# Block pair kernel: the second half of the middle norm one unit later and cut in three, its spreads after it, and five weight tiles bounded by a one-column sum on TensorE

## What is computed

```python
    x = x + jnp.einsum('bsf,fd->bsd', f, w_ff2[l])      # end of block 1
    x = rms_norm(x, final_g)                            # middle norm
    # block 2, first layer
    h = _rms(x, norm_g)                                 # a_norm_2
    proj = h @ w_in                                     # 1024 x 4096
    q, k, v, g = jnp.split(proj, [DA_QK, 2 * DA_QK, 2 * DA_QK + DA_V], axis=-1)
    qs = [_rope_partial(_rms(q[:, :, :, c], q_norm), pos) for c in range(2)]
    ks = [_rope_partial(_rms(k[:, :, :, c], k_norm), pos) for c in range(2)]
```

## Time and profile before

| | us |
|---|---|
| time, median of 3 runs | 2532.23 (2521.53 to 2538.52) |
| time of the profiled execution | 2530.41 |
| its span | 2528.6 |
| TensorE busy | 2363.5 |
| VectorE busy | 1519.4 |
| ScalarE busy | 968.2 |
| GpSimd busy | 216.0 |

### The profile page before, as it was taken

One profiled execution on the slowest core, in us unless ns is written; L12 is line 12 of the kernel. 1 busy time (PEld: TensorE's weight loads), 2 busy tenths in 40 slices (PEclk: granted clock), 3 DMA queues, 4 the chain that ended last, 5 costly groups with the idle time before them and its releaser, 6 DMA issues.

```text
span 2528.6 us, 30214 instructions
## 1 busy us (share of the span) xinstructions
PE 2363.5 (93%) x12840; PEld 1252.4 (50%) x12840; DVE 1519.4 (60%) x1962; ACT 968.2 (38%) x1383; POOL 216.0 (9%) x263
## 2 busy tenths in 40 slices
PE   6999999999999999898999777899999998888899
PEld 4445444444444444344444455654444445666764
DVE  6898755644454455777631488965534307888862
ACT  5245334212121212323321466732323116777741
POOL 0001030000000002324201101022000000000000
PEclk9999999999999999898999899999999998999999
DMA  4010011110101010121011000021130100000021
GB/s 177 34 67 34 1 34 63 70 67 34 67 34 67 34 67 34 36 101 67 34 67 34 1 1 1 8 93 34 67 133 34 68 1 34 1 1 1 1 84 50
DMA packets 50326, 116.00 MB, mean 46 GB/s; under 512 B 2386, under 2 KB 7819, under 8 KB 49808
## 3 DMA queue, kind: packets, MB, share of 16 engines
q1 hardware_dynamic: 48456, 105.40, 11.8%
q10 hardware_dynamic: 1736, 8.68, 0.8%
HBM read 101.49 MB, written 12.58 MB: 45 GB/s over the span
## 4 chain that ended last, share of the span: by engine, by line
PE 76%; DVE 13%; ACT 6%; issue 3%; DMA 1%; POOL 1%; ACTq 0%; DVEq 0%; POOLq 0%
PE PS L72 72%; ACT RG L81 4%; PE PS L75 3%; DVE R L93 2%; DVE R L101 2%; DVE RG L107 2%; DVE mx L110 2%; DVE RG L101 2%; ACT OV L84 1%; DVE scl L110 1%; DMA RG<-in_a_w_in 1%; DVE RG L93 1%; DVE oss L110 1%; ACT R L81 1%; ACT OV L81 0%
## 5 line engine op out<-in xcount | busy, mean ns | idle before, releaser
L72 PE MATMUL PS<-R,RG 128*128 128x512 f16 (+1 forms) x5472 | 1167.6, 375 | 10.2 <-DVE RG L101 4.7
L72 PEld LDWEIGHTS PS<-R,RG 128*128 128x128 f16 (+1 forms) x5472 | 543.4, 103 | 631.8 <-issue 14.5
L72 PE MATMUL PS<-RG,R 128*128 128x512 f16 x2880 | 634.6, 381 | 4.5 <-DVE R L101 4.0
L72 PEld LDWEIGHTS PS<-RG,R 128*128 128x128 f16 x2880 | 282.7, 98 | 337.8 <-issue 7.5
L81 ACT ACTIVATE R<-PS,scl 128x512 f32<-128x512 f32 (+1 forms) x192 | 126.8, 687 | 716.1 <-PE PS L72 616.3
L101 DVE SCALAR_TENSOR_TENSOR R<-PS,scl,R 128x512 f32<-128x512 f32 (+1 forms) x208 | 148.7, 746 | 149.2 <-PE PS L72 124.1
L107 DVE TENSOR_TENSOR_SCAN RG<-RG 128x127 f32<-128x127 f32 (+7 forms) x128 | 168.6, 1345 | 110.4 <-ACT RG L81 110.1
L72 PE MATMUL PS<-R,OV 128*128 128x64 f32 (+2 forms) x1456 | 194.5, 286 | 34.9 <-DVE R L93 32.8
L101 DVE SCALAR_TENSOR_TENSOR RG<-RG,scl 128x4096 f16<-128x4096 f32 (+1 forms) x43 | 188.7, 4389 | 52.2 <-ACT RG L81 52.2
L72 PEld LDWEIGHTS PS<-R,OV 128*128 128x128 f32 x1456 | 180.6, 199 | 45.1 <-DVE R L93 39.3
L75 PE MATMUL PS<-ident,RG 128*128 128x128 f32 x864 | 148.5, 289 | 47.1 <-ACT OV L84 23.9
(11 more groups left out here) (120 smaller groups left out, 1546.7 us busy)
## 6 DMA issues: line engine op xcount, KB each, us to landing
RG<-in_w_ff SPq DMA_DIRECT2D x16, 2048.0 KB, 8.1
RG<-in_a_w_in SPq DMA_DIRECT2D x8, 2048.0 KB, 8.5
RG<-in_w_in SPq DMA_DIRECT2D x4, 2048.0 KB, 9.6
xspill<-R ACTq DMA_DIRECT2D x2, 4096.0 KB, 15.3
RG<-in_w_kv SPq DMA_DIRECT2D x4, 2048.0 KB, 8.0
RG<-in_b_w_in SPq DMA_DIRECT2D x4, 2048.0 KB, 7.9
R<-in_x SPq DMA_DIRECT2D x8, 512.0 KB, 9.1
RG<-in_w_out SPq DMA_DIRECT2D x2, 2048.0 KB, 7.7
```

Source lines behind the costliest of these rows:

```text
L72: return self.engine.matmul(*a, **k) if self.engine else Nothing()
```

## The change

1. Spread `final_g` of half 0 leaves the end of block 1 (j = 12) for unit 7; its diagonal goes from j = 11 to unit 5, its eight `final_x` from j = 12, 13 to units 7 and 8.
2. Half 1: sums from unit 1 to 3, spread `a_norm_2` from unit 2 to 4, `final_h` from units 2, 3 (four and four) to units 3, 4, 5 (four, two, two), spread `final_g` from unit 6 to 10, `final_x` from units 6, 7 to 10, 11, the spill from unit 9 to 12.
3. Tile 23 is converted four products later (j = 12 instead of 8).
4. Tiles 24, 25, 26 and 27 are measured and converted at other places. Measurements, before: units 5, 10, 16, 24; after: units 6, 14, 22, 30. Conversions, before: after units 6, 12, 17, 25; after: units 9, 17, 25 and the second vv unit. Tiles 28 and 29 move from the first and second unit of their vv half to the sixth and seventh of the first, and the fourth and fifth of the second.
5. For tiles 24 to 27 and 30 (`BOUNDED`) GpSimd's reduction over the partitions is gone. TensorE multiplies the 128 peaks by `ones` (one column) into a PSUM bank of the ring, which gives their sum in each partition, an upper bound of the largest; VectorE's `power` reads it from there. The factor can be smaller by up to seven bits than before. TensorE does this at the start of the unit at whose end the tile is converted, and waits there for the measurement.

```diff
@@ -174,12 +174,13 @@
 for _i in range(7, 38):
     if _i not in (28, 29):
         MEASURE[_i, 1], CONVERT[_i, 2] = _i + 2, _i + 2
-for _i in (7, 8, 19, 20, 21, 22, 23, 30, 31, 32, 33, 35):
+for _i in (7, 8, 19, 20, 21, 22, 23, 24, 25, 26, 27, 30, 31, 32, 33, 35):
     del MEASURE[_i, 1], CONVERT[_i, 2]
 for _j, _m, _c in ((7, None, (6, 7)), (8, (7, 2), (7, 3)), (9, (7, 6), (7, 7)), (10, (8, 6), (8, 8)),
-                   (21, (19, 1), (19, 2)), (22, (19, 6), (20, 1)), (23, (20, 7), (21, 9)),
-                   (24, (23, 2), (23, 3)), (25, (22, 7), (23, 5)), (32, (30, 7), (30, 8)),
+                   (21, (19, 1), (19, 2)), (22, (19, 6), (20, 1)), (23, (20, 7), (21, 13)),
+                   (24, (23, 3), (22, 6)), (25, (23, 7), (24, 2)), (26, (24, 7), (25, 2)),
+                   (27, (25, 7), (26, 2)), (28, (26, 6), (26, 7)), (29, (27, 4), (27, 5)), (32, (30, 7), (30, 8)),
                    (33, (31, 4), (32, 4)), (34, (32, 8), (33, 1)), (35, (33, 5), (33, 6)),
                    (37, (35, 3), (35, 8))):
     CONVERT[_c] = _j
@@ -187,6 +188,8 @@
         MEASURE[_m] = _j
 LOW = {(_i, _at + 1): _j for (_i, _at), _j in CONVERT.items() if (_i, _at) != (35, 8) and (_i, _at) != (30, 8)}
 LOW[36, 1], LOW[31, 1] = 37, 32
+
+BOUNDED = (24, 25, 26, 27, 30)
 def block_kernel(nc, A):
@@ -492,6 +495,17 @@
                                       start=(k == 0 and ws + hs == 0), stop=(k == 7 and hs == 1))
                 mm.then_inc(*full.up(*key))
                 last_product[i] = key
+
+            def bound(i):
+
+                b = banks.take(("bound", i))
+                e.wait_ge(*sig("w_peak").at(i))
+                e.wait_ge(*banks.free(("bound", i)))
+                e.matmul(b[:, 0:1], ones[:, :], w_col(i, 0), start=True, stop=True).then_inc(*full.up("bound", i))
+
+            def feed(i, use):
+                if CONVERT.get((i, use)) in BOUNDED:
+                    bound(CONVERT[i, use])
             def h_ready(name, n):
@@ -717,8 +731,6 @@
                     sums("final", 0)
                 if j == 8:
                     spread("a_norm_2", 0)
-                if j == 12:
-                    spread("final_g", 0)
                 down(key)
@@ -731,21 +743,25 @@
                 mm.then_inc(*full.up("qt", u))
             for u, (which, c, t) in enumerate(qk_units):
-                if u == 1:
+                if u == 3:
                     sums("final", 1)
-                if u == 2:
+                if u == 4:
                     spread("a_norm_2", 1)
-                if u == 6:
-                    spread("final_g", 1)
+                if u in (7, 10):
+                    spread("final_g", u // 10)
+                feed(22 + 2 * which + c, t + 1)
                 product_n(22 + 2 * which + c, t, ("qk", u), ready=h_ready("a_norm_2", t // 4))
                 if u > 2:
                     qk_turn(u - 3)
             for c in range(2):
                 for t in range(NT):
+                    feed(26 + c, t + 1)
                     product_n(26 + c, t, ("vv", c, t))
                     if c == 0 and t < 3:
                         qk_turn(29 + t)
             for t in range(NT):
+                if t == 2:
+                    bound(30)
                 for c in range(2):
                     product_n(28 + c, t, ("gg", t, c))
@@ -960,10 +976,13 @@
                 e.tensor_reduce(w_col(i, 0), w_raw(i), AX.X, ALU.max,
                                 apply_absolute_value=True).then_inc(*sig("w_peak").up(i))
-            def power(inv, f, top, bits=14):
-
-                e.tensor_scalar(inv, top, TINY, 2.0 ** -bits, ALU.max, ALU.mult).then_inc(*step.up())
-                e.wait_ge(*step.last())
+            def power(inv, f, top, bits=14, key=None):
+
+
+                done = sig("bank_dve") if key else step
+                up = banks.empty([key], done, *key) if key else step.up()
+                e.tensor_scalar(inv, top, TINY, 2.0 ** -bits, ALU.max, ALU.mult).then_inc(*up)
+                e.wait_ge(*done.last())
                 e.tensor_scalar(inv.bitcast(I32), inv.bitcast(I32), EXPONENT, None,
                                 ALU.bitwise_and).then_inc(*step.up())
                 e.wait_ge(*step.last())
@@ -973,6 +992,11 @@
                 return e.scalar_tensor_tensor(low, src, f, high, ALU.mult, ALU.subtract)
             def factor(i):
+                if i in BOUNDED:
+                    key = ("bound", i)
+                    e.wait_ge(*full.at(*key))
+                    power(w_inv(i), w_col(i, 2), banks.ap(key)[:, 0:1], key=key).then_inc(*sig("w_factor").up(i))
+                    return
                 e.wait_ge(*sig("w_top").at(i))
                 power(w_inv(i), w_col(i, 2), w_col(i, 1)).then_inc(*sig("w_factor").up(i))
@@ -1453,10 +1477,6 @@
                     diagonal(("norm2", 1), ("a_norm_2", 0), 8)
                 if 8 <= j < 12:
                     final_h(0, range(2 * j - 16, 2 * j - 14))
-                if j == 11:
-                    diagonal(("a_norm_2", 0), ("final_g", 0), 0)
-                if j in (12, 13):
-                    final_x(0, range(4 * j - 48, 4 * j - 44))
                 down(key, j % 8 + 9)
@@ -1492,15 +1512,20 @@
                                 ALU.subtract).then_inc(*banks.empty([key], sig("bank_dve"), *key))
             for u in range(32):
-                if u == 1:
+                if u == 3:
                     final_factors(1)
-                    diagonal(("final_g", 0), ("a_norm_2", 1), 12)
-                if u in (2, 3):
-                    final_h(1, range(4 * u - 8, 4 * u - 4))
-                if u == 4:
-                    diagonal(("a_norm_2", 1), ("final_g", 1), 4)
-                if u in (6, 7):
-                    final_x(1, range(4 * u - 24, 4 * u - 20))
+                    diagonal(("a_norm_2", 0), ("a_norm_2", 1), 12)
+                    final_h(1, range(4))
+                if u in (4, 5):
+                    final_h(1, range(2 * u - 4, 2 * u - 2))
+                if u == 5:
+                    diagonal(("a_norm_2", 1), ("final_g", 0), 0)
+                if u in (7, 8):
+                    final_x(0, range(4 * u - 28, 4 * u - 24))
+                if u == 8:
+                    diagonal(("final_g", 0), ("final_g", 1), 4)
+                if u in (10, 11):
+                    final_x(1, range(4 * u - 40, 4 * u - 36))
                 qk_norm(u)
                 if u > 2:
                     qk_low(u - 3)
@@ -2099,11 +2124,12 @@
                 e.dma_start(xs, R1[:, :]).then_inc(*sig("spilled").up(by=16))
             for u in range(32):
-                if u == 1:
+                if u == 3:
                     final_roots(1)
-                if u in (2, 3):
-                    final_h(1, range(4 * u - 8, 4 * u - 4))
-                if u == 9:
+                    final_h(1, range(4))
+                if u in (4, 5):
+                    final_h(1, range(2 * u - 4, 2 * u - 2))
+                if u == 12:
                     spill()
                 qk_square(u)
                 if u > 2:
@@ -2392,8 +2420,6 @@
                     feed(26 + c, t + 1)
             e.wait_ge(*sig("constants").at("subln"))
             for t in range(NT):
-                if t == 1:
-                    measure(30)
                 gg = GG[:, t, :].rearrange("p (h e) -> p h e", h=8)
                 e.wait_ge(*sig("bank_act").at("gg", t, 1))
                 e.tensor_tensor(gg, gg, subln.rearrange("p (o e) -> p o e", o=1).broadcast_to([P, 8, P]),
```

## The result

| | before | after |
|---|---|---|
| time, median (lowest to highest) | 2528.90 us (2521.53 to 2538.52, 6 runs) | 2501.88 us (2497.67 to 2513.61, 6 runs) |
| profiled execution: time, span | 2530.41, 2528.6 | 2500.57, 2498.8 |
| TensorE busy | 2363.5 | 2352.5 |
| GpSimd busy | 216.0 | 213.5 |

The ratio is 0.9885, with a 95% interval of 0.9864 to 0.9907: the changed kernel is 27.0 us faster, 1.15% (forecast: 2505 us, 26.8 us less than before).

What follows compares the result with a forecast made beforehand. TensorE was taken to bound the kernel, its four gaps being worth 30.6 us. 30.6 - 3.0 - 0.6 - 1.1 + 0.9 = 26.8 us off the profiled 2530.4 gives 2503.6, median 2505 us, range 2494 to 2519.

Steps and rivals of the forecast that it cites:

- The price of the gaps: TensorE's four gaps between j = 12 and unit 31, with slower rows behind them: 14.2, 11.0, 3.8, 1.6, together 30.6 us.
- Part 1, the first gap goes whole: At j = 12 to 15 and units 0 to 2, nothing else comes late; the whole 14.2 us goes.
- VectorE late at both `final_g` spreads: Units 7 and 10: TensorE waits for VectorE's diagonals, 3.0 us in all, plus 0.6 for the clock.
- The other gaps go by themselves: Transposes behind GpSimd's rotations: none waits any more after the tiles move; all of 11.0 + 3.8 + 1.6 us goes.
- The clock behind a wait: Clock loss at the `final_g` spreads, 0.6 us: a gap of 1.53 cost nothing, one of 2.05 cost 1.7.
- The bounds: Five one-column products on TensorE add 0.23 us each, 1.1 in all, between 0.5 and 2.5 if weights are fetched late.
- Tile 25 "lands 8.5 us later ... is measured in unit 14 by 1133": Tile 25's load starts about 1114 and is measured in time, wanted at unit 17 at 1137.
- the second rival: Tile 25's load still meets the spill, takes 19.6 us; its bound waits 1 to 2, with clock 3: 2508 us. Chance 0.10.
- The banks: Ring shifted by five: no cost at the first attention's scores, gain of 0.9 us at the second attention's start.
- VectorE was not late by more than 1.74 us anywhere (2518): Rival: GpSimd and VectorE slow each other, both `final_g` spreads wait 11 us more in all; 2518 us. Chance 0.16.
- TensorE's waits were what bounded: Rival claimed the opposite: what follows the q and k units has its own pace, gain given back; 2532 us. Chance 0.05.
- (slower): Rival: the later spill holds up VectorE's `qk_norm` from unit 16, landing after 1181; time above 2535 us. Chance 0.03.

Runs made afterwards that it cites:

- late_x: Changed kernel with both `final_g` spreads and their `final_x` one unit later (units 8 and 11), spill after unit 13: 2498.29 us, ratio 0.9894 to the kernel before.
- early_x: Changed kernel with `final_g` of half 0 spread in unit 2, half 1 in unit 8, spill after unit 10; run twice: 2505.71 and 2500.18 us.
- tiles_only: Kernel before with only tiles 24 to 30 measured, bounded and converted as in the change; norm, spill and tile 23 as before: 2513.82 us, ratio 0.9952.
- gpsimd_again: Changed kernel with GpSimd's reductions again for tiles 24 to 27 at the change's places, tile 30 still bounded: 2506.14 us, ratio 0.9911 to the kernel before.
- early_x_gpsimd: early_x with GpSimd's reductions again for tiles 24 to 27, tile 30 still bounded: 2498.92 us, ratio 0.9863 to the kernel before.
- norm_only: Kernel before with only the norm's parts, spill and tile 23 moved as in the change, tiles 24 to 30 as before: 2516.39 us, ratio 0.9950.
- banks_only: Kernel before with only the bank ring moved on by one at the five places where the change puts a bound: 2530.47 us, ratio 1.0003.
- change_again: Changed kernel run once more, unaltered: 2499.73 us, ratio 0.9883 to the kernel before.

## Why the prediction was right

**The price of the gaps** (30.6 us): right. Without the 1.45 us at the scores the stretch is 26.0 us shorter, and it holds 3.54 us of new waits, 0.3 of slower rows at them and 0.73 for five bounds: 30.6. What the sum puts on top of the waits (1.06 and 0.89, 0.52 and 2.29, 0.06 and 1.69) are rows behind them less the same work undisturbed. The granted clock there was 0.50 in the spread behind the first gap and 0.92 in the 48 products, 0.50 and 0.70 in the transposes and the unit behind the second, 0.76 in the unit behind the third, and 1.00 behind the fourth.

**Part 1, the first gap goes whole** (14.2): right. The window 1013.41 to 1049.67 has no idle time and a clock of 1.00; the sums stand at 1049.67, forecast 1050.6.

**VectorE late at both `final_g` spreads** (3.0, and 0.6 for the clock): right in kind, too high in size. TensorE was at the first at 1074.9 (forecast 1075.7) and waited 1.74 us (1.3), at the second at 1094.7 (1095) and waited 0.53, below the lower end of 0.8 (by the prediction's own terms that wait would lie between 1.0 and 3.7, 1096 and 1098.7 less 1095). The clock cost 0.1 us at each and not 0.6. That VectorE is what comes late is shown twice: late_x wants both diagonals a unit later, early_x makes the first before unit 0 and wants the second in unit 8, and both waits go.

**The other gaps go by themselves** (16.4): right, and tiles_only shows it alone. Two of its reasons have to be told apart. It named the reduction that is gone and the three units between measurement and conversion; gpsimd_again and early_x_gpsimd show that the new places alone bring the 16.4 us down to 1.6 and 2.4. I had not asked which of the two pays. Not tried were the bounds at the old places, and the single moves of the tiles and of the norm one by one, so which of the moves is needed isn't shown.

**The clock behind a wait**: the step "a gap of 1.53 cost nothing, one of 2.05 cost 1.7" read a limit into two rows that isn't there. In norm_only a gap of 2.54 us cost nothing (granted clock 1.00 behind it), and one of 1.13 us shortly behind one of 6.08 was followed by a unit of 7.05 (0.76).

**The bounds** (5 x 0.23 = 1.1): 0.15 each, 0.7 in all, within its 0.5 to 2.5; that late weights would bring it to 2.5 was the author's estimate and is not shown. Tile 24, the tight one, was measured by 1086.5, wanted at 1088.8, and waited for nothing.

**Tile 25 "lands 8.5 us later ... is measured in unit 14 by 1133"**: wrong. The load took 19.4 us, the measurement ended at 1136.9, and the bound waited 1.27 us. That is the second rival with its mechanism and place; it happened beside the forecast, and not in its stead, since its price was 1.27 us and not 3. The row for it was there: the same load beside the same spill had taken 19.6. Setting it at 8.5 all the same, since it now starts some microseconds ahead, was the author's estimate, and so was the chance of 0.10 for the rival; no run shows a load that starts so little ahead of the spill and lands that soon. It landed at 1132.4, the spill at 1133.1, though the load is half the size and was issued 3.3 us ahead. Had the two shared equally, the load would have landed some 11 us after its issue (an estimate: 3.3 us at its pace alone, then half of what the two moved together until 1133.1); the trace does not agree. Early_x and late_x, where the two are issued 11.7 and 8.8 us apart, give it 8.8 and 9.5 us.

**The banks** (0.9): right. 0.9 from ScalarE's last row to the first sigmoid, in the change and in banks_only.

**The rivals that did not come.** VectorE was not late by more than 1.74 us anywhere (2518); TensorE's waits were what bounded, since the 26 us of the stretch are still there at the end (2532); the spill landed at 1133.1, and in late_x at 1134.3, with nothing waiting for it, far from the 1150 from which it would cost (slower). The room was smaller than the prediction thought, which had unit 16 come 17 us earlier, at 1137: its product starts at 1129.9, 23 us earlier than before.

**The signs.** There is no gap at j = 12 and none in front of a transpose, the q and k units end at 1221.6 (1222), GpSimd has no reduction from 1020 to 1250 us, and both `dg` waits are released by VectorE, the second shorter than the 1 to 2 us named. Two signs did not come: the load of tile 25 took 19.4 us and not under 13, and its bound has a gap ahead of it. A gap at unit 17 released by a measurement was named as a sign of being wrong; it stood there, with 1.27 us and not over 4.

**The sum**: the errors were 0.7 and 0.4 too much for VectorE and the clock, 0.4 for the bounds, and 1.4 too little for tile 25, its slower row included. They cancel to 0.1 us, which is luck. The median came out 3.1 us under the forecast, well within 2494 to 2519. That is hardly a term of the sum: the forecast stood on the kernel before at 2532.23 us, the median of three runs, and six give 2528.90, 3.3 lower, while the two medians lie 27.0 apart and 26.8 were forecast. How much of a time is the second attention, whose clock differs from run to run, six runs don't settle. The chance for "faster" came from its parts as 0.53 (three quarters of 0.66, a third of 0.10) and not 0.54.

## What to carry to other kernels

When an engine's measurement holds up a chain, first ask how far its result is from its use: moving the tiles, with three units between measurement and conversion, took away all but 1.6 to 2.4 us of the 16.4 that the gaps behind the reductions cost. Replacing the reduction too is worth 1.7 us more where its replacement waits for nothing, and nothing where it waits itself. When two such kernels are compared, take out of the stretch first what is hidden behind it, here the 1.45 us at the scores. Two large transfers that meet are priced by the trace of the same pair, not by the duration of either alone (here 19.4 us for the load beside the spill, 8.8 apart from it); if x can be finished two units earlier, the spill is out of the load's way. And where one late stretch of a kernel varies by 13.7 us with the granted clock, read changes of a few microseconds from the length of their own stretch, which here repeated to 0.14 us in the change and to some 2 us in the kernel before.

## What the runs showed of the hardware

- **A load beside a spill.** In the six profiles in which the 4 MB spill is issued 0.7 to 3.3 us after the load of 2 MB, the load takes 18.5 to 19.6 us and the spill 16.7 to 17.4. In the six in which the two are issued 8.7 us or more apart, in either order, it is 8.6 to 9.5 and 11.2 to 13.0. The small transfer pays more (about 10 us) than the large one (about 5).
- **The length of a wait does not set the clock behind it.** 2.05 us were followed by a unit of 7.03 us at a granted clock of 0.76 (before), 2.54 (norm_only) and 1.74 (banks_only) by one of 5.34 at 1.00.
- **Two patterns of the granted clock in the second attention.** With TensorE busy for 20.00 of every 20 us at a clock of 1.00 from 1960 to 2060 us in both change_again and early_x, the second attention takes 314.3 or 327.9 us. Over the twelve profiles it takes 314 to 317 us in nine, whose first 20 us lie at a clock of 0.74 (the kernel before) or 0.83 to 0.85, and 327 to 328 us in three, whose first 20 us lie at 0.64. Early_x shows both in two runs. What chooses it stays open.
- **A reduction's surroundings.** GpSimd's reduction over the partitions takes 0.38 us. In the twelve for tiles 24 to 27 of before, gpsimd_again and early_x_gpsimd it does nothing else for 6.7 to 7.6 us behind it, and for 5.7 to 6.2 us ahead of it in the ten in which it doesn't wait for the peaks longer.
